# Order of work in a fused two-network kernel: the opening, two gated norm passages, and the last norm beside a GLU

## What is computed

```python
def first_block(x, ...):                      # two layers
    for layer in range(2):
        hn = rmsnorm(h, mix_norm[layer])
        h = h + (moba_nsa_mixer(hn, ...) if layer == 0 else fox_mixer(hn, ...))
        h = h + sqrelu_mlp(rmsnorm(h, mlp_norm[layer]), mlp_w1[layer], mlp_w2[layer])
    return rmsnorm(h, final_norm)

def second_block(x, c, ...):                  # one layer; sh, sc, gt from silu(c) @ w_ada + b_ada
    n = modulate(rmsnorm_2(h, g_ffn1), sh1, sc1)
    h = h + 0.5 * gt1 * swiglu(n, w1_gate, w1_up, w1_down)
    n = modulate(rmsnorm_2(h, g_mix), sh2, sc2)
    h = h + gt2 * hybrid_mixer(n, w_in, w_pool, pool_scale, w_out)
    n = modulate(rmsnorm_2(h, g_ffn2), sh3, sc3)
    h = h + 0.5 * gt3 * swiglu(n, w2_gate, w2_up, w2_down)
    return rmsnorm_2(h, g_final)
```

## Time and profile before

| | us |
|---|---|
| median of 3 runs | 1099.05 |
| lowest, highest | 1098.44, 1100.7 |
| the profiled execution | 1098.95 |
| its span, first to last instruction | 1097.2 |
| TensorE busy | 1076.2 (98%) |
| VectorE busy | 778.6 (71%) |
| ScalarE busy | 660.4 (60%) |
| GpSimd busy | 115.5 (11%) |
| mean granted TensorE clock | 0.996 |

### The profile page before, as it was taken

The page is one execution under the profiler, slowest core; times in us unless marked ns, Lnnn a source line. Parts: engine busy times, 40 slices in busy tenths (PEclk is TensorE's granted clock), DMA queues, the critical chain, the costliest instruction groups (busy, mean ns, idle before and its releaser), DMA issues.

```text
span 1097.2 us, 15918 instructions
## 1 busy us (share of the span) xinstructions
PE 1076.2 (98%) x6098; PEld 918.3 (84%) x6098; DVE 778.6 (71%) x1261; ACT 660.4 (60%) x1067; POOL 115.5 (11%) x209
## 2 busy tenths in 40 slices
PE   8999999999999999999999999999999999999997
PEld 7898788888888998888888788888878978888885
DVE  6767667777786776687676777887875766565566
ACT  6667676565666776766565754354475766444443
POOL 2033101010100531020000000110000200000000
PEclk9999999999999999999999999999999999999999
DMA  9842348878864643687778467768545344555551
GB/s 341 298 158 79 115 156 326 304 289 306 300 217 173 212 140 113 217 306 279 255 277 312 154 227 289 294 244 312 188 165 183 131 154 173 192 191 183 185 183 64
DMA packets 40619, 238.30 MB, mean 217 GB/s; under 512 B 4661, under 2 KB 5845, under 8 KB 17632
## 3 DMA queue, kind: packets, MB, share of 16 engines
q1 hardware_dynamic: 26784, 188.81, 48.3%
q0 software_dynamic: 13040, 47.85, 11.7%
q10 hardware_dynamic: 720, 0.62, 0.2%
HBM read 236.15 MB, written 1.11 MB: 216 GB/s over the span
## 4 chain that ended last, share of the span: by engine, by line
PE 81%; DVE 9%; ACT 5%; issue 3%; DMA 1%; POOL 0%; DVEq 0%; ACTq 0%
PE bank L1570 20%; PE bank L1539 13%; PE bank L1541 13%; PE bank L1540 13%; PE bank L1571 10%; PE bank L1694 2%; DVE w_lo L1070 2%; PE bank L1758 1%; ACT w_hi L699 1%; PE bank L1740 1%; DVE ada_raw L1300 1%; PE bank L1732 1%; PE bank L1588 1%; PE bank L1589 1%; PE bank L1592 1%
## 5 line engine op out<-in xcount | busy, mean ns | idle before, releaser
L1570 PE MATMUL bank<-a_two,w_hi 128*128 128x512 f32 x1088 | 386.9, 399 | 0.8 <-DVE w_lo L1070 0.8
L1070 DVE TENSOR_TENSOR w_lo<-raw,w_hi 128x2048 fp32r<-128x2048 f32 x122 | 278.4, 2303 | 107.2 <-ACT w_hi L699 107.1
L1571 PE MATMUL bank<-a_two,w_lo 128*128 128x256 f32 x1088 | 305.5, 281 | 0.0
L699 ACT ACTIVATE w_hi<-raw 128x2048 fp32r<-128x2048 f32 x122 | 232.2, 1910 | 63.5 <-DMA raw<-in_stream 63.4
L1570 PEld LDWEIGHTS bank<-a_two,w_hi 128*128 128x128 f32 x1088 | 204.5, 188 | 51.0 <-issue 1.4
L1571 PEld LDWEIGHTS bank<-a_two,w_lo 128*128 128x128 f32 x1088 | 205.7, 189 | 1.7
L1539 PE MATMUL bank<-w_lo,hid_hi 128*128 128x512 f32 x432 | 169.6, 393 | 0.3 <-DVE w_lo L1070 0.2
L1540 PE MATMUL bank<-w_hi,hid_lo 128*128 128x512 f32 x432 | 168.7, 390 | 0.0
L1541 PE MATMUL bank<-w_hi,hid_hi 128*128 128x512 f32 x432 | 168.6, 390 | 0.0
L871 ACT ACTIVATE cross<-bank 128x256 f32<-128x256 f32 x136 | 51.5, 381 | 186.2 <-PE bank L1571 186.1
L1059 DVE TENSOR_TENSOR w_lo<-raw,w_hi 128x1024 fp32r<-128x1024 f32 x104 | 125.5, 1229 | 22.3 <-ACT w_hi L688 22.2
(11 more groups left out here) (231 smaller groups left out, 1478.4 us busy)
## 6 DMA issues: line engine op xcount, KB each, us to landing
raw<-in_stream SPq DMA_DIRECT2D x173, 1024.0 KB, 5.0
ada_raw<-in_ada POOLq DMA_DIRECT2D x72, 512.0 KB, 5.3
cmpw<-in_stream SPq DMA_DIRECT2D x4, 1024.0 KB, 8.1
rel_band<-rel_scratch POOLq DMA_DIRECT2D x2, 1024.0 KB, 7.2
cum_row<-cum_scratch POOLq DMA_DIRECT2D x4, 512.0 KB, 4.8
gate_row<-gate_scratch POOLq DMA_DIRECT2D x3, 512.0 KB, 5.8
h<-in_x SPq DMA_DIRECT2D x2, 512.0 KB, 4.3
raw<-in_stream SPq DMA_DIRECT2D x2, 512.0 KB, 7.0
```

Source lines behind the costliest of these rows:

```text
L699: nc.scalar.activation(w_hi[:, u % RING, :], raw[:, u % RING, :], ACT.Copy).then_inc(hi_ready, 2)
L1070: nc.vector.tensor_tensor(w_lo[:, u % RING, :], raw[:, u % RING, :], w_hi[:, u % RING, :].bitcast(F32), ALU.subtract).then_inc(lo_ready, 2)
L1570: nc.tensor.matmul(ps[bank][:, 0:2 * T], wh[:, k, cols_], a_two[:, :, k, :], start=k == 0, stop=False)
L1571: ins = nc.tensor.matmul(ps[bank][:, T:2 * T], wl[:, k, cols_], a_hi[:, k, :], start=False, stop=k == KT - 1)
```

## The change

It has three parts.

1. The opening. ScalarE turns chunk 3 of both tiles and rounds unit 3, in two halves, ahead of its wait for the small product. GpSimd waits for the sixth half of w_lo before its two memsets.
2. The passages gmix and gf2 get an order of their own, `gated_turn`, on ScalarE and on VectorE. VectorE, not ScalarE, multiplies tile 1 by its inverse root, in two halves. VectorE's shift of chunk 3 of tile 0 comes behind the last add instead of before it, and the first mean of tile 1 right after. ScalarE takes the root of tile 1 before it rounds the half unit, not after. `turn_rows` counts the scaled pieces by two counters accordingly.
3. Beside glu0 the last norm is spread: one half at each of j = 2, 3, 4, 5.

```diff
+        def scaled_by_dve(name, t):
+            return name == "mix0" or (name in ("gmix", "gf2") and t == 1)
+        def scaled_before(name, t):
+            rows_ = [(n, k) for n in NORMS for k in range(TT)]
+            mine = scaled_by_dve(name, t)
+            return (2 if mine else 3) * sum(scaled_by_dve(*r) == mine for r in rows_[:rows_.index((name, t))])
...
             pool.wait_ge(pool_step, 1)
+            pool.wait_ge(lo_ready, 6)
             zeros(slice(0, 6), 0)
...
+            def gated_turn(name, gain, shift):        # ScalarE
+                squares(name, 0)
+                round_half()
+                scale(name, 0)
+                turned(name, 0, gain, shift, (0, 1))
+                square_half(name, 1, 0)
+                turned(name, 0, gain, shift, (2,))
+                square_half(name, 1, 1)
+                root(name, 1)
+                turned(name, 0, gain, shift, (3,))
+                round_half()
+                turned(name, 1, gain, shift)
...
             round_half()
             round_half()
+            for t in range(TT):
+                turned("mix0", t, gain0, chunks=(3,))
+            round_half()
+            round_half()
             act.wait_ge(rel_rows, 1)
             nc.scalar.activation(rrow[:, :], ps[4][0:16, 0:REL], ACT.Copy).then_inc(rel_rows_sb, 1)
-            for t in range(TT):
-                turned("mix0", t, gain0, chunks=(3,))
             advance(FIRST["v_even"] + 4)
...
+            def gated_turn(name, sums, gain, shift, gate):        # VectorE
+                for k in range(2):
+                    add(name, sums, gate, 0, k)
+                inverse_root(name, 0)
+                rest_half()
+                add(name, sums, gate, 1, 0)
+                shift_chunk(name, 0, 1, gain, shift)
+                turned(name, 0, gain, shift, (0, 1), False)
+                add(name, sums, gate, 1, 1)
+                shift_chunk(name, 0, 3, gain, shift)
+                first_mean(name, 1)
+                turned(name, 0, gain, shift, (2,))
+                inverse_root(name, 1, True)
+                scale(name, 1)
+                turned(name, 0, gain, shift, (3,))
+                rest_half()
+                turned(name, 1, gain, shift)
...
-                        if name == "glu0" and j in (2, 4):
-                            first_norm_root(j // 2 - 1)
-                            last_norm(j // 2 - 1)
+                        if name == "glu0" and 2 <= j < 6:
+                            if j % 2 == 0:
+                                first_norm_root(j // 2 - 1)
+                            last_norm(j // 2 - 1, j % 2)
...
             def turn_rows(name, t):
-                n = NORMS.index(name)
                 for c in range(4):
-                    if c < 3 and n > 0:
-                        pe.wait_ge(rows_scaled_act, 6 * (n - 1) + 3 * t + c + 1)
-                    elif c % 2 == 0:
-                        pe.wait_ge(rows_scaled, 2 * t + c // 2 + 1)
+                    if scaled_by_dve(name, t):
+                        if c % 2 == 0:
+                            pe.wait_ge(rows_scaled, scaled_before(name, t) + c // 2 + 1)
+                    elif c < 3:
+                        pe.wait_ge(rows_scaled_act, scaled_before(name, t) + c + 1)
```

More of the change, by code:

```diff
@@ L1000, in _ @@
             glu("glu0")
-            norm_turn("gmix", gainc[:, KT:2 * KT], modc[:, 3 * KT:4 * KT])
+            gated_turn("gmix", gainc[:, KT:2 * KT], modc[:, 3 * KT:4 * KT])
             advance(FIRST["uv_dil"] + 4)
@@ L1027, in _ @@
             act.wait_ge(gain_ready, 3)
-            norm_turn("gf2", gainc[:, 2 * KT:3 * KT], modc[:, 6 * KT:7 * KT])
+            gated_turn("gf2", gainc[:, 2 * KT:3 * KT], modc[:, 6 * KT:7 * KT])
             glu("glu1")
@@ L1087, in add, with first_mean, inverse_root @@
                     nc.vector.tensor_tensor(to, to, tok[:, t, half], ALU.add).then_inc(h_ready, 1)
-            def inverse_root(name, t):
+            def first_mean(name, t):
+                dve.wait_ge(sumsq, squares_before(name, t) + 1)
+                nc.vector.tensor_scalar(stat[:, 2, t:t + 1], stat[:, 0, t:t + 1], EPS[name], None, ALU.add).then_inc(mean_ready, 1)
+            def inverse_root(name, t, first_taken=False):
                 n = NORM[name]
                 first, v, y, b = (stat[:, i, t:t + 1] for i in (2, 4, 5, 6))
-                dve.wait_ge(sumsq, squares_before(name, t) + 1)
-                nc.vector.tensor_scalar(first, stat[:, 0, t:t + 1], EPS[name], None, ALU.add).then_inc(mean_ready, 1)
+                if not first_taken:
+                    first_mean(name, t)
                 dve.wait_ge(mean_ready, n + t + 1)
@@ L1151, in first_norm_root, with shift_chunk, turned @@
                 chain(nc.vector.scalar_tensor_tensor(out=f[:, 13:14], in0=f[:, 15:16], scalar=1.5, in1=f[:, 14:15], op0=ALU.add, op1=ALU.mult))
-            def turned(name, t, gain, shift=None, chunks=(0, 1, 2, 3)):
+            def shift_chunk(name, t, c, gain, shift):
                 m = TURN[name] + 4 * t
+                dve.wait_ge(bank_turned, m + c + 1)
+                if t == 1:
+                    dve.wait_ge(act_split, m - 4 + c + 1)
+                for kt in (2 * c, 2 * c + 1):
+                    ins = nc.vector.tensor_scalar(shifted[:, c, kt % 2, :], ps[TURN_BANKS[name][t][c]][:, (kt % 2) * P:(kt % 2 + 1) * P],
+                                                  gain[:, kt:kt + 1], shift[:, kt:kt + 1], ALU.mult, ALU.add)
+                ins.then_inc(rows_shifted, 1)
+            def turned(name, t, gain, shift=None, chunks=(0, 1, 2, 3), shifts=True):
                 ts = slice(t * P, (t + 1) * P)
                 for c in chunks:
[L1158 to L1166, removed]
+                    if shift is not None and c < 2 and shifts:
+                        shift_chunk(name, t, 2 * c + 1, gain, shift)
                     dve.wait_ge(act_high, split_no(name, t, c))
@@ L1273, in hidden_part, with last_norm @@
                                         ALU.subtract).then_inc(hid_ready, 1)
[L1275 to L1280, removed]
+            def last_norm(t, k):
+                half = slice(512 * k, 512 * k + 512)
+                nc.vector.scalar_tensor_tensor(out=h[:, t, half], in0=h[:, t, half], scalar=fin[:, t, 13:14], in1=row[:, half],
+                                               op0=ALU.mult, op1=ALU.mult).then_inc(h_final, 1)
             def gains(names):
@@ L1490, in _ @@
             dve.wait_ge(h_final, 4)
-            norm_turn("gmix", "glu0", gainc[:, KT:2 * KT], modc[:, 3 * KT:4 * KT], gate_row)
+            gated_turn("gmix", "glu0", gainc[:, KT:2 * KT], modc[:, 3 * KT:4 * KT], gate_row)
             advance(FIRST["uv_dil"] + 4)
@@ L1510, in _ @@
             dve.wait_ge(gate_landed, 32)
-            norm_turn("gf2", "out_dil", gainc[:, 2 * KT:3 * KT], modc[:, 6 * KT:7 * KT], gate_row)
+            gated_turn("gf2", "out_dil", gainc[:, 2 * KT:3 * KT], modc[:, 6 * KT:7 * KT], gate_row)
             glu("glu1")
```

## The result

| | before | after |
|---|---|---|
| median, us | 1098.7 (6 executions) | 1093.32 (6 executions, 1092.09 to 1094.24) |
| ratio of the two | | 0.995, 95% interval 0.9938 to 0.9963 |
| the profiled execution | 1098.95 | 1092.9 |
| its span | 1097.2 | 1090.7 |
| outside the span (median of all executions) | 1.81 | 2.17 |

The change makes the kernel 0.5% faster: 5.4 us by the medians, 6.05 between the two profiled executions. The forecast was 1094.35, with a range of 1091.8 to 1097.1.

A forecast was written before the change was run, and what follows sets the result against it. TensorE, busy 98% of the span, was taken as the bound, so only its waits and half-clock stretches pay. Opening 2.28, gmix 0.97, gf2 0.67 and glu0 0.70 sum to 4.62: 1098.95 to 1094.35 us, range 1091.8 to 1097.1.

The forecast's parts named there:

- rival 1: Opening and gf2: fewer clock falls; 1092.8 us if one goes, 1091.2 if both; chance 0.25.
- Memsets: Opening: with memsets moved, VectorE's row scaling takes 0.48 us instead of 1.16, so TensorE gains 0.68.
- The moved memsets cost nothing: Opening, about 20.3 to 23.4 us: memsets beside VectorE's subtractions and w_lo cost nothing; even 1.4 us would be covered.
- Chunk 3 and unit 3 before rrow: Opening: ScalarE no longer waits first for the relative-bias matmul, so TensorE's lost 1.60 us before unit 3 all go.
- Rival 2: First network: transfers set the pace and the gains of 1.60 and 0.7 are given back; 1096.6 us, chance 0.10.
- The clock, in the forecast unchanged: Opening and behind gf2: as many half-clock stretches as before, each costing about 1.6 us; chance 0.52.
- Gmix: Gated passage: uv_dil's second pair of matmuls starts at 819.65 instead of 820.62, gain 0.97 us; TensorE bounds what follows.
- Gf2: Same chain 86.9 us later: the next matmul, of first_rows, starts at 906.58 instead of 907.25, gain 0.67 us.
- VectorE multiplies: Gated passages: VectorE scales rows 128 to 255, taken as 0.48 us per half, bounds 0.47 to 1.16.
- rival 3: Gated passages: VectorE's scaling is stretched as in the opening, losing 0.4 and 0.7 us; 1097.1 us, chance 0.08.
- Glu0: Turns 2 and 4: spreading the last norm makes w_lo earlier; gain 0.7 us, bounds 0 and 1.1.
- Rival 4: Gmix, gf1 and gf2: TensorE falls to half clock behind split idle pieces; up to 1102.4 us, chance 0.05.

The follow-up runs named there:

- e10: The changed kernel itself, unaltered, run again on one chip beside its ScalarE-scaling variant; median 1093.71 us, ratio 0.9947 to before.
- e2: Kernel before with only GpSimd's two memsets moved behind the sixth w_lo half; 1097.10 us against 1098.84, ratio 0.9990.
- e4: Kernel before with only the last norm spread over four turns of glu0; 1097.93 us against 1098.84, ratio 0.9990.
- e3: Kernel before with only the two gated passages changed, VectorE's scaling included; 1096.25 us against 1098.84, ratio 0.9978.
- e1: Kernel before with only the opening's two edits: memsets moved, chunk 3 and unit 3 ahead of rrow; 1095.39 us against 1098.84, ratio 0.9972.
- e8: Changed kernel with two table loads moved to glu0, passages' half w_lo earlier, uv_dil's first unit in halves, glu1's halves split three and one; 1090.88 us.
- e5: Changed kernel with ScalarE again multiplying rows 128 to 255 in the gated passages, new order kept; 1091.92 us, ratio 0.9948 to before.
- e11: Changed kernel with ScalarE scaling in the gated passages, run on one chip beside the changed kernel (1093.71 us); 1092.01 us.

## Why the prediction was right, point by point

The median came at 1093.32: inside the range of 1091.8 to 1097.1, but 1.0 under the forecast of 1094.35, just below the forecast's own 1093.4, and nearer to rival 1's 1092.8. The forecast held for as many clock falls as before, and one pair of traces meets that condition: e10, the changed kernel with two half-clock stretches, took 1094.62 us, against the 1098.95 of before with two. That is 4.33 us for the 4.62 of the sum, with the reserve that the two executions may be from different chips. The pair before and after, less its two falls, gives only 3.3. So the mechanisms of the steps held, their sum was somewhat too large, and fewer falls made up for it. That the two errors, of opposite sign, leave the median within 1.0 is in part luck. By its steps:

- **Memsets, 0.68 predicted.** The scaling took the length foreseen, and the transposes came 0.56 earlier (0.48 in e2, 0.40 to 0.73 over the eleven kernels with this edit). The scalings themselves began at 9.43 to 9.76 in these, 9.49 in before, which is scatter: 9.55 and 9.60 in e4 and e3, with the memsets in their old place. Slightly over.
- **The moved memsets cost nothing.** So it was. 2.29 and 1.13 beside memsets of 1.38, as without them in before. The rule cited there from the Trainium skill, page "SBUF — State Buffer", section "SBUF: two separate sides", that an instruction with two SBUF inputs is held up only by a GpSimd instruction that reads SBUF, agrees with the 2.29, of an instruction whose inputs both lie there. What the stretched form costs shows in e4, where the old place of the memsets makes the pair 1.55, against 0.88.
- **Chunk 3 and unit 3 before rrow, 1.60.** 1.67 in after, 1.74 in e1. The slack was as worked out, and the even mixer gave nothing back: 3.57 at 30 us, 3.60 at 605. Rival 2 falls.
- **The clock, in the forecast unchanged.** This is the largest miss. In the pair of traces both falls are gone, which is 2.7 of its 6.05. But the number of falls varies in both kernels: 30 executions of before have mean clocks of 0.993 to 0.998, 0.9956 on average, and 11 of the changed kernel 0.9975. The difference is 0.0019 of some 1095 us, or 2.1 us; a stretch of 3.4 us at half clock makes 1.7 of that, so the change takes away 1.2 stretches on average, worth 1.7 us. This is an estimate from these rows, and a rough one: the mean clock also counts a half clock behind the last matmuls, of 2.6 us in after and 5.3 in e10. The table above, read as shares, gives 1.3 fewer (3 of 4 less 0 of 10 in gf2, 2 of 3 less 1 of 11 in the opening). The other steps make the rest, 3.6 of the 5.3 between the two means. Rival 1 is right in part: what changes is how often a fall comes, and the prediction, which held the number equal, took the earlier trace rows for a fixed pattern where it was one draw. A fall costs 1.36, and not the 1.6 that was worked out. The rule cited at rival 1 from the Trainium skill, page "TensorE: Matmul & The Clock Gate", section "What's actually happening", that the activity monitor runs free of the kernel, fits what e10 and after show.
- **Gmix, 0.97.** 1.26 at the pair of products that the step named, with a wait of 0.30 ahead of it where 0.5 was foreseen. What failed in this step is "what follows is then bound by TensorE": VectorE's w_lo of the first unit of uv_dil came too late. With the new wait of 0.19 at 822.56 the lead falls from 4.79 to 4.35, and 0.70 was left. e8 shows it from the other side.
- **Gf2, 0.67.** 0.97 at its first product, 2.07 at the end, of which 1.36 is the fall; the 0.7 that remain are the term.
- **VectorE multiplies.** The bound on a stretched scaling didn't come true, 0.88 for the pair in both passages, and rival 3 falls. But the step credited the exchange with part of the gain, and e5 and e11 show that the order does it all. ScalarE's pieces do start 0.40 later there, once the two leads at 804 are made equal, and so do the transposes; but VectorE writes the half w_lo in the meantime, and by the first unit of uv_dil both ways have gained the same 0.70 to 0.74.
- **Glu0, 0.7.** 0.67 in after and in e4, with the wait of turn 2 gone and one of 0.37 left in turn 4, as worked out.
- **Missing from the sum.** 0.36 us outside the span, which went against the change in every execution and hid part of what the clock gave. The 0.6 at 608 is no term of the change: it stands in after, and in e10, the same program, the lead grows by 0.38 there.
- **Rival 4.** Gmix never fell in 14 traces; gf1 fell in 7 of them, for one stretch each time. No slowing came of it. The prediction named a half clock at gf1 as a sign of being wrong. It came in e10, but also in e1 and e2, which leave the passages as they were, so it tells nothing of the change.

## What to carry to other kernels

When a wait is taken away, look at the next one due on the same engine and price the gain there: gmix gained 1.26 where it was repaired and kept 0.70, and the rest was kept only with the following unit in halves (e8). Before work is handed to another engine, price the new order with the old engine: here the order made the gain, and with the next unit as the limit the exchange brought nothing that was kept and cost 0.36 us outside the span. A half-clock stretch in one trace is one draw; compare its place over several executions before it enters a sum. The same holds for a short wait: the 0.81 at 608 was gone in another execution of the same program.

## What the runs showed of the hardware

- The same program's granted clock differs between executions by half-clock stretches of 3.4 us, each of which costs 1.36 us. It goes with much of this kernel's scatter: of 30 executions of before on one chip, two at a mean clock of 0.998 took 1096.4 us on average, and two at 0.993 took 1100.5. It isn't all of it: on another chip one at 0.998 took 1099.03.
- Two passages of before have nearly the same idle time, 1.44 to 1.47 us. The later one (gf2) had a fall behind it in 3 traces of 4, and the earlier (gmix) in none of 4. What tells them apart the runs don't show.
- Two VectorE instructions in place of three ScalarE ones, in a passage in the middle of the program, made the time outside the span longer: by 0.24 us with one such passage (gf2), and by 0.36 with two. The cause wasn't found.
